# An attention stage's exponentials ahead of its probability copies, and small tables built later

## The reference, cut to what matters

```python
# layer 0 ("ab"): two kinds of heads over the same tokens
#   a: windowed attention with a bias and a sink;  b: the difference of two softmaxes, scaled by lambda
# layer 1 ("cd"): latent attention (c) and a windowed grid attention with a bias (d)
x = x + 0.5 * mx[2] * swiglu_2(modulate(rms_norm(x), mx[0], mx[1]), *ffn1)
h = modulate(rms_norm(x), mx[3], mx[4])
y, y_c = mix_window_diff(h, hc, ab_w_in[i], ab_w_out[i], a_q_norm[i], a_k_norm[i], a_sink[i], ...)
x = x + mx[5] * y
```

## Time and profile before

| | us |
|---|---|
| median of 3 runs | 2675.45 |
| lowest, highest | 2673.09, 2677.14 |
| the profiled execution's time | 2677.14 |
| the profiled execution's span | 2675.3 |
| PE busy | 2525.6 (94%) |
| DVE busy | 1346.7 (50%) |
| ACT busy | 1022.1 (38%) |
| mean granted TensorE clock | 0.971 |

### The profile page before, as it was taken

The page is one execution under the profiler, slowest core; times in us unless marked ns, Lnnn a source line. Parts: engine busy times, 40 slices in busy tenths (PEclk is TensorE's granted clock), DMA queues, the critical chain, the costliest instruction groups (busy, mean ns, idle before and its releaser), DMA issues.

```text
span 2675.3 us, 36277 instructions
## 1 busy us (share of the span) xinstructions
PE 2525.6 (94%) x15262; PEld 2155.1 (81%) x15262; DVE 1346.7 (50%) x2221; ACT 1022.1 (38%) x1633; POOL 0.2 (0%) x4
## 2 busy tenths in 40 slices
PE   7999999999989999989788999998999988888998
PEld 6998779989977888878566888886888877768998
DVE  4747554554454333357876333334333446646554
ACT  4534444444333222136552222213222226543542
POOL 0000000000000000000000000000000000000000
PEclk8999999999999999999989999999999999989999
DMA  7986743499842323335002333332333326401554
GB/s 266 303 263 208 231 127 103 126 337 330 313 155 87 101 96 95 98 116 188 24 1 71 96 101 95 95 101 73 98 99 95 96 86 183 147 9 64 174 183 133
DMA packets 145476, 372.23 MB, mean 139 GB/s; under 512 B 20234, under 2 KB 65570, under 8 KB 145186
## 3 DMA queue, kind: packets, MB, share of 16 engines
q1 hardware_dynamic: 144882, 368.21, 42.6%
q10 hardware_dynamic: 432, 1.69, 0.2%
HBM read 368.71 MB, written 1.15 MB: 138 GB/s over the span
## 4 chain that ended last, share of the span: by engine, by line
PE 87%; DVE 8%; ACT 3%; issue 1%; DMA 1%; SPq 0%; ACTq 0%; DVEq 0%
PE psum L347 75%; PE psum L725 3%; PE psum L1548 2%; PE psum L1519 1%; DVE normed_raw L533 1%; DVE normed_lo L546 1%; PE psum L1536 1%; PE psum L1450 1%; DVE weights_lo L295 1%; PE psum L1138 1%; PE psum L939 1%; PE psum L1150 1%; PE psum L494 1%; ACT weights_hi L289 1%; DVE arena L1615 0%
## 5 line engine op out<-in xcount | busy, mean ns | idle before, releaser
L295 DVE TENSOR_TENSOR weights_lo<-weights_raw,weights_hi 128x1024 fp32r<-128x1024 f32 (+3 forms) x547 | 657.5, 1212 | 517.4 <-ACT weights_hi L289 514.6
L347 PE MATMUL psum<-normed_hi,weights_hi 128*128 128x256 f32 (+1 forms) x2560 | 864.2, 338 | 36.5 <-DVE normed_lo L546 24.6
L347 PE MATMUL psum<-normed_lo,weights_hi 128*128 128x256 f32 (+1 forms) x2560 | 850.3, 332 | 0.0
L347 PE MATMUL psum<-normed_hi,weights_lo 128*128 128x256 f32 (+1 forms) x2560 | 849.9, 332 | 0.0
L289 ACT CAST weights_hi<-weights_raw 128x1024 fp32r<-128x1024 f32 (+3 forms) x547 | 562.9, 1035 | 375.3 <-DMA weights_raw<-in_w_down 259.2
L347 PEld LDWEIGHTS psum<-normed_hi,weights_hi 128*128 128x128 f32 x2560 | 491.2, 192 | 111.0 <-issue 46.9
L347 PEld LDWEIGHTS psum<-normed_lo,weights_hi 128*128 128x128 f32 x2560 | 492.5, 192 | 44.1 <-issue 1.2
L347 PEld LDWEIGHTS psum<-normed_hi,weights_lo 128*128 128x128 f32 x2560 | 492.0, 192 | 44.3
L347 PE MATMUL psum<-hidden_hi,weights_hi 128*128 128x512 f32 x528 | 205.6, 389 | 0.0
L347 PE MATMUL psum<-hidden_lo,weights_hi 128*128 128x512 f32 x528 | 205.5, 389 | 0.0
L347 PE MATMUL psum<-hidden_hi,weights_lo 128*128 128x512 f32 x528 | 205.5, 389 | 0.0
(11 more groups left out here) (254 smaller groups left out, 2788.7 us busy)
## 6 DMA issues: line engine op xcount, KB each, us to landing
weights_raw<-in_w_gu SPq DMA_DIRECT2D x220, 512.0 KB, 3.5
weights_raw<-in_w_down SPq DMA_DIRECT2D x110, 512.0 KB, 3.5
arena<-in_w_mod SPq DMA_DIRECT2D x72, 512.0 KB, 7.1
weights_raw<-in_w_x SPq DMA_DIRECT2D x24, 512.0 KB, 4.7
resid<-in_w_mod SPq DMA_DIRECT2D x24, 512.0 KB, 6.8
normed_raw<-in_w_mod SPq DMA_DIRECT2D x24, 512.0 KB, 7.1
under_normed_hi<-in_w_mod SPq DMA_DIRECT2D x24, 512.0 KB, 7.6
weights_raw<-in_w_qk SPq DMA_DIRECT2D x24, 512.0 KB, 4.0
```

What stands on the lines that cost most here:

```text
L295: ve.tensor_tensor(w_lo[:, c % RING, a], w_raw[:, c % RING, a], w_hi[:, c % RING, a].bitcast(F32), ALU.subtract).then_inc(lo_ready, 1)
L347: last = te.matmul(out, a, b, start=start and n == 0, stop=stop and n == 2)
```

## The change

Two things are moved; no instruction is added or taken away.

In `Attend`, ACT's copy of unit i-2 now stands behind the exponentials of unit i instead of ahead of them, and DVE's weights of unit i-1 now stand ahead of the copy of unit i-2.

`GainTables` and `Lambda` of layer 0 no longer stand between the two projections of the first feed-forward part. They stand behind that part and behind the norm that follows it, just ahead of the attention's projections. `GainTables` of layer 1 stands behind the feed-forward part's second projection and ahead of the norm.

```diff
             def scalar(self, act, step, i):
-                if 2 <= i < len(self.units) + 2:
-                    j, u = i - 2, self.units[i - 2]
-                    act.wait_ge(aa_turned, self.base + j + 1)
-                    if j >= 2:
-                        act.wait_ge(aa_pv, self.base + j - 1)
-                    w = len(u.values[0]) * P
-                    se.copy(self.turned[:, j % 2, 0, 0:w], psum[:, 4, 0:w]).then_inc(aa_copied, 1)
                 if i < len(self.units):
                     ...
                     last.then_inc(aa_exp, 1)
+                if 2 <= i < len(self.units) + 2:
+                    ...
+                    se.copy(self.turned[:, j % 2, 0, 0:w], psum[:, 4, 0:w]).then_inc(aa_copied, 1)
 
             def vector(self, dve, step, i):
                 if i < len(self.units):
                     self.maxima(dve, i)
+                if 1 <= i <= len(self.units):
+                    self.weights(dve, step, i - 1)
                 if 2 <= i < len(self.units) + 2:
                     ...
-                if 1 <= i <= len(self.units):
-                    self.weights(dve, step, i - 1)
@@ layer 0
-        tables = GainTables(("aq", "ak", "bq", "bk"), *rope64, HD, [tables64[g] for g in ("aq", "ak", "bq", "bk")])
-        alone(*first[:2], tables, Lambda(), *first[2:], norm,
+        alone(*first, norm, GainTables(("aq", "ak", "bq", "bk"), *rope64, HD,
+                                       [tables64[g] for g in ("aq", "ak", "bq", "bk")]), Lambda(),
               Merged(beside(steps_of(*ab_main[1:]), side)))
@@ layer 1
-        alone(*chain[:-1], GainTables(("cqr", "ckr"), *rope32, ROPE, [tables32[g] for g in ("cqr", "ckr")]), chain[-1])
+        alone(*chain, GainTables(("cqr", "ckr"), *rope32, ROPE, [tables32[g] for g in ("cqr", "ckr")]))
```

More of the change, by code:

```diff
@@ L1570, in scalar @@
                     last.then_inc(aa_exp, 1)
+                if 2 <= i < len(self.units) + 2:
+                    j, u = i - 2, self.units[i - 2]
+                    act.wait_ge(aa_turned, self.base + j + 1)
+                    if j >= 2:
+                        act.wait_ge(aa_pv, self.base + j - 1)
+                    w = len(u.values[0]) * P
+                    se.copy(self.turned[:, j % 2, 0, 0:w], psum[:, 4, 0:w]).then_inc(aa_copied, 1)
             def vector(self, dve, step, i):
```

## The result

| us | before | after | after, a second series | forecast |
|---|---|---|---|---|
| median | 2676.3 (4 runs) | 2699.84 (4 runs) | 2695.72 (5 runs, before 2676.2) | 2690 |
| lowest, highest | 2673.09, 2677.64 | 2696.54, 2700.87 | 2695.03, 2699.45 | 2681 to 2699 |
| ratio, 95% interval | | 1.0087 [1.007, 1.0102] | 1.008 [1.0068, 1.0093] | |
| profiled execution, its span | 2677.14, 2675.3 | 2701.74, 2700.0 | span 2697.7 | |

The direction was right and the size was not: +23.5 us in the first series (2699.84 - 2676.3), +19.5 in the second, where +14.9 was forecast. The first series lies 0.84 us above the range, the second inside it. The mean of the granted clock fell from 0.971 to 0.966.

The account below looks back on a forecast made before the run. PE was taken to bound the kernel (busy 94% of the span), with DVE and ACT partly pacing layer 0's attention. Terms 7.1 + 0 + 7.0 + 0.8 = +14.9 us on median 2675.45 gave 2690.3, taken as 2690; range 2681 to 2699.

Parts of the forecast that it names:

- Part 1: Layer 0's tables and lambda behind the norm: fourth weight chunk 4.7 us late plus 2.4 us lower clock, +7.1 us.
- Part 2: Layer 1's tables ahead of the norm: they fit in DVE's idle 1.28 us, 0, bounds 0 and +0.3 us.
- Part 3: New order in layer 0's attention: PE's transposes wait for ACT's later copy, +7.0 us, bounds +1 and +13.
- Part 4: New order in layer 1's attention: three turns' copies come later and PE waits, +0.8 us, bounds 0 and +1.5.
- The new gaps cost clock as well: Rival: PE's new gaps in layer 0's attention also lower its clock, 6 us more, 2696.3 us; chance 0.22.
- Only the tables: Rival: late transposes in layer 0's attention disappear in DVE's own pace, 2684.4 us; chance 0.18.
- the copies were the brake: Rival: ACT's copies standing first held up exponentials in attention; new order gains 15 us, 2667.6 us; chance 0.03.
- no change: Rival: first projection's stall absorbed later in the stage, attention's by DVE; within 5 us, about 2678; chance 0.07.

Follow-up runs that it names:

- tables_filled: Kernel before with only tables and lambda moved, plus 28 identity transposes on PE ahead of its wait for the fourth weight chunk: ratio 1.0015, median 2679.67 us.
- order_only: Kernel before with only the attention's new order on ACT and DVE, both layers, tables and lambda unmoved: median 2689.88 us, ratio 1.0049.
- filled_gaps: Changed kernel plus 14 identity transposes on PE ahead of the late-copy transposes, once per tile of layer 0's attention: 2690.94 us, ratio 1.0058.
- act_only: Kernel before with only ACT's copy moved behind the exponentials, DVE in the old order, tables unmoved: median 2691.49 us, ratio 1.0058.

## Why the prediction was right or wrong, step by step

- **Part 1, +7.1: right.** Measured +7.3 (115.48 to 122.77), of it 4.7 wait as read from the tables' old place, and 2.7 clock, as tables_filled shows by taking it away. The 2.4 was 12 x 0.2; the rows' own 0.44 and 0.21 give 12 x 0.23, 2.8.
- **Part 2, 0: right.** The tables lie in the idle time ahead of the norm's read.
- **Part 3, +7.0: measured +18.2; this is the step that failed.** The mechanism of the stalls was right: transposes released by ACT's late copy, at the first a units of each tile, and only there with waits of 1.99 to 2.74 us. The sum of the stalls was nearly right too: PE's idle time grew by 7.8 us in the stage, 7.4 in order_only. My shares by tile were not. By the starts of the transposes, less each stage's start, the changed kernel is 2.5 us late at tile 0's, 6.4 at tile 1's, 10.4 at tile 2's, 15.9 at tile 3's and 18.2 at the end, with the largest step (5.5) between tile 2's and tile 3's, where the 19 us at the lower level lie. What the sum left out is the clock: 10.4 us more busy time in the first profile, 7.2 in the second (103.33 - 96.09) and 7.3 in order_only. Even the upper bound, 1.5 us at each of four places, was too small. So about half of the stage's 18.2 us is what the waits cost by themselves and about half what the clock took behind them, as filled_gaps shows (8.0 and 10.1).
- **Why I left it out.** I argued from one gap, 2.73 us ahead of 1298.38, that the expected gaps were shorter and so free. The trace of before held a counter-example 76 us later, within the 1 to 2.5 us of idle time that I expected: a wait of 2.28 us in front of tile 3's first transposes (1374.10) and 6 us at 0.50 behind it, with PE busy throughout. Had I asked for the stage in stretches of 6 us instead of one stretch of 120, it would have stood there, and 3 us for each of four places, 12 in all, would have been the natural price. It would have been near the sum (10.4 and 7.2), not right in the single places, which lost from nothing to some 10 us.
- **Part 4, +0.8: right for the waits; what the clock adds is not settled.** Between the first two profiles it is +0.1, by chance: before's first profile had the slow output projection. Over all of them, the eight profiles with ACT's old order have 122.7 to 123.2 us six times and 125.8 twice in layer 1, the six with the new order 125.9 to 126.6 five times and 124.17 once. The means are 123.6 and 125.8, +2.1. Of this PE's idle time is +1.0 (12.2 to 12.3 us in the attention in all eight, 13.0 to 13.4 in the six), which is the forecast's term, and +1.2 is busy time with the same instructions, about half of it behind the output projection's first matmul: there the clock is below full in all six and in four of the eight. Whether the new order brings that or chance does, these profiles do not settle.
- **The rivals.** "The new gaps cost clock as well", 2696.3 with a chance of 0.22, is what happened: its time lies between the medians of the two series, 2695.72 and 2699.84. That it fits so well is in part luck, since its price of the clock, 6 us, was too small as well: 7.2 to 10.4 us were lost. "Only the tables" (2684.4) falls with order_only's +14.1, "the copies were the brake" with act_only's +15.7, "no change" with both. The 2.8 us of the earlier trace rows, read there as PE's waits for an exponential, are its weight loads' (PEld).
- **The range** ended at 2699, since I took the clock's upper bound from 1.5 us a place.
- **Sum.** From the medians, tables +7.6 and order +14.1 give 21.7, and the whole gave 23.5 and 19.5. Within the intervals the parts add up.

## What to carry to other kernels

Where PE is the bound and stalls of 2 us or more are added, price each of them twice: the wait, and the work behind it at the lower clock, taken from several waits of that size in the same stage, the longest low stretch among them, not from the mean clock or from one sample. In this kernel the second price was as large as the first. An engine that waits for a late operand with a finished short job queued behind it (here ACT's copy behind exponentials that wait for DVE) should do the short job first; that alone was worth 14 to 16 us here. And before an order is tuned further, look whether a few cheap matmuls in the pauses buy more.

## What the runs showed of the hardware that I had not expected

- Tile 2's wait of 1.99 us was followed by 19 us at a granted clock of 0.50, with PE busy for 18.96 us or more of them, in three of four profiles. In the fourth, act_only's, it was some 3 us, and 18.79 us at 0.50 stood behind tile 3's wait of 1.99 us instead.
- The same instructions behind the same wait can get either clock: 0.57 and 1.00 behind 2.07 us in tile 1, 0.71 and 1.00 in layer 1's output projection. Profiles of one kernel so differ by 3 us in a stage, and one profile cannot size such a term.
- Transposes of the identity kept the clock up: 14 of them in 1.75 us, in tile 2's wait, left 1.00 for the next 10.4 us, where 0.50 had stood for 19. Sixteen in a wait of 5 us behind the norms shortened nothing: the first matmuls then ran at full clock, but behind a wait of 0.56 us for DVE the clock was low again (0.80 us for one matmul).
